# Order and engines of the last mixing steps in a fused attention, convolution and hierarchical MoE step

## The reference

```python
def hier_moe(h, w_rg, b_rg, w_re, b_re, w_gate, w_up, w_down):
    ...
    g_star = jnp.argmax(lg, axis=-1)                     # one of 4 groups per token
    ...
    top_p, top_i = lax.top_k(pe, TOP_K)                  # 2 of its 8 experts
    w = p_group * top_p / jnp.sum(top_p, axis=-1, keepdims=True)
    ...
    y = grouped_experts(x, e_idx, w.astype(x.dtype), w_gate, w_up, w_down)
    return y.reshape(b, t, d)

# grouped_experts: for the rows of each expert e
#   (silu(xblk @ w_gate[e]) * (xblk @ w_up[e])) @ w_down[e], times the token's weight, summed per token
# and the caller adds the residual: xp = xp + hier_moe(...), xs = xs + hier_moe(...)
```

## Time and profile before

| what | value |
|---|---|
| median of 3 runs | 1435.9 us (1434.64 to 1437.3) |
| the profiled execution's own time | 1436.35 us |
| its span, first to last instruction | 1434.4 us |
| PE (TensorE matmul) busy | 1242.1 us, 87% of the span |
| VectorE (DVE) busy | 433.2 us, 30% |
| ScalarE (ACT) busy | 217.4 us, 15% |
| bytes moved | 503.63 MB, mean 351 GB/s over the span |
| mean granted TensorE clock | 0.947 |

### The profile page before, as it was taken

The page is one execution under the profiler, slowest core; times in us unless marked ns, Lnnn a source line. Parts: engine busy times, 40 slices in busy tenths (PEclk is TensorE's granted clock), DMA queues, the critical chain, the costliest instruction groups (busy, mean ns, idle before and its releaser), DMA issues.

```text
span 1434.4 us, 21171 instructions
## 1 busy us (share of the span) xinstructions
PE 1242.1 (87%) x8998; PEld 675.9 (47%) x8998; DVE 433.2 (30%) x863; ACT 217.4 (15%) x462; POOL 45.4 (3%) x33
## 2 busy tenths in 40 slices
PE   9999999999999998997877778796787787777887
PEld 8888888888788862331222232132232122213223
DVE  4322127674211143322311321231222231132142
ACT  3111232322000043110101111011011010101101
POOL 0000003140000001000000000000000000000000
PEclk9999999999999999998989998899999898999899
DMA  9975443669399359999999999999999999999997
GB/s 342 348 227 183 140 133 121 206 206 340 88 349 413 121 182 427 417 425 435 427 433 432 430 433 431 431 431 431 431 432 432 430 432 432 432 432 430 433 426 317
DMA packets 101202, 503.63 MB, mean 351 GB/s; under 512 B 9294, under 2 KB 79638, under 8 KB 86182
## 3 DMA queue, kind: packets, MB, share of 16 engines
q1 hardware_dynamic: 89346, 494.86, 85.0%
q10 hardware_dynamic: 11812, 8.14, 1.8%
HBM read 496.42 MB, written 6.59 MB: 351 GB/s over the span
## 4 chain that ended last, share of the span: by engine, by line
PE 53%; DMA 44%; DVE 2%; ACT 1%; issue 0%; DVEq 0%; ACTq 0%; SPq 0%
PE bank L735 31%; DMA ring<-in_w_gate 16%; DMA ring<-in_w_up 15%; DMA ring<-in_w_down 12%; PE bank L1023 9%; PE bank L1058 3%; PE bank L958 2%; PE bank L1076 1%; DVE xa L1913 1%; PE bank L1073 1%; DMA xa<-in_x_prompt 1%; PE bank L746 0%; PE bank L826 0%; PE bank L776 0%; PE bank L1084 0%
## 5 line engine op out<-in xcount | busy, mean ns | idle before, releaser
L1023 PE MATMUL bank<-ring,bc 128*32 128x512 f32 x2040 | 272.4, 669 | 113.7 <-DMA ring<-in_w_gate 61.9
L735 PE MATMUL bank<-bc,ring 128*128 128x264 f32 x1536 | 350.8, 387 | 1.3 <-ACT cat L1261 1.3
L735 PEld LDWEIGHTS bank<-bc,ring 128*128 128x128 f32 x1536 | 288.2, 190 | 51.5 <-issue 2.3
L1023 PEld LDWEIGHTS bank<-ring,bc 128*32 128x32 f32 x2040 | 63.7, 118 | 288.2 <-issue 146.5
L1913 DVE TENSOR_TENSOR xa<-xa,bank 128x512 f32<-128x512 f32 x128 | 79.3, 682 | 153.0 <-PE bank L1076 146.6
L735 PE MATMUL bank<-cat,ring 128*128 128x264 f32 x512 | 114.9, 387 | 0.0
L735 PEld LDWEIGHTS bank<-cat,ring 128*128 128x128 f32 x512 | 97.0, 190 | 17.7 <-issue 1.3
L1927 DVE COPY bc<-bank 128x512 f32<-128x512 f32 x32 | 22.1, 691 | 234.6 <-PE bank L1023 234.6
L1058 PE MATMUL bank<-ring,cat 128*32 128x512 f32 x480 | 67.2, 684 | 22.4 <-DMA ring<-in_w_down 22.4
L958 PE MATMUL bank<-cat,bc 128*32 128x512 f32 x512 | 61.3, 597 | 13.5 <-DVE xa L1913 13.5
L1487 ACT ACTIVATE bc<-bank 128x512 f32<-128x512 f32 x32 | 19.1, 597 | 289.6 <-PE bank L1023 289.6
(11 more groups left out here) (300 smaller groups left out, 1023.5 us busy)
## 6 DMA issues: line engine op xcount, KB each, us to landing
ring<-in_w_gate SPq DMA_DIRECT2D x27, 4096.0 KB, 31.8
ring<-in_w_up SPq DMA_DIRECT2D x27, 4096.0 KB, 31.6
ring<-in_w_down SPq DMA_DIRECT2D x26, 4096.0 KB, 32.7
ring<-in_w_in SPq DMA_DIRECT2D x23, 2048.0 KB, 15.3
ring<-in_w_up SPq DMA_DIRECT2D x10, 2048.0 KB, 12.9
ring<-in_w_gate SPq DMA_DIRECT2D x9, 2048.0 KB, 15.4
ring<-in_w_down SPq DMA_DIRECT2D x9, 2048.0 KB, 16.1
ring<-in_w_out SPq DMA_DIRECT2D x8, 2048.0 KB, 16.5
```

Source lines behind the costliest of these rows:

```text
L735: m = pe.matmul(bank[n % 3][:, 0:T], w[:, k, (i % TPU) * P:(i % TPU + 1) * P], src[:, k, :], start=n_k == 0, stop=n_k == KT - 1)
L1023: m = pe.matmul(bank[b][c * C:(c + 1) * C, :], xeT[j % 2][:, k, :], wx, start=i == 0 and x < 4, stop=i == 1 and x >= 4, skip_group_check=True)
```

## The change

Four things are changed, the arithmetic aside from rounding order stays as it was.
- end_residual takes the half too. end_residual(1, 2) is taken from behind the third down's second half to ahead of it, and two new ones, (0, 0) and (0, 1), stand beside it. The pair (0, 0) so starts from the residual in its banks (END_ROWS).
- ScalarE moves the pair (0, 0) out of its banks with two plain copies (move_rows(0, 0), between its two copies of bank 2), as it does with (1, 1); VectorE's two adds of (0, 0) go. row_moved counts 4 per group, and the waits on it follow.
- mix_last(1) is split by t; sample_last(1) stands between its halves, and VectorE adds "s" ahead of both adds of (1, 0).
- The stores: SP issues the sample pieces 0, 1 and 2 ahead of y columns 1024 to 1535, which leave in one DMA of 512 KB; ScalarE's queue issues the sample piece 3 alone. There are eight DMAs in place of nine.

```diff
--- before.py
+++ after.py
@@ -131,9 +131,10 @@
 PIECE = 256
 END_BANKS = {(0, 0): 0, (0, 1): 6, (1, 0): 6, (1, 1): 3}
 END_ORDER = {0: (2, 3, 0, 1), 1: (0, 1, 2, 3)}
-END_ADDS = [(0, 1, 0), (0, 1, 1), (0, 0, 0), (0, 0, 1), (1, 0, 0), "s", (1, 0, 1)]
+END_ADDS = [(0, 1, 0), (0, 1, 1), "s", (1, 0, 0), (1, 0, 1)]
+END_ROWS = ((0, 0), (1, 1))
 END_ADD = {x: n + 1 for n, x in enumerate(END_ADDS)}
-END_MIX = {(0, 1): 1, (0, 0): 2, (1, 0): 3, (1, 1): 4, "s": 5}
+END_MIX = {(0, 1): 1, (0, 0): 2, "s": 3, (1, 0): 4, (1, 1): 5}
 NEND = len(END_ADDS)
 
 Y_ORDER = [(0, g) for g in range(4)] + [(1, g) for g in range(4)] + [(2, 0), (2, 1), None, (2, 2), (2, 3)]
@@ -646,20 +647,18 @@
 
             y = outs["y_prompt"].rearrange("o (t p) d -> p (o t) d", p=P)
             every = npass * (NG * NEND)
-            for n, last in ((1, (0, 1, 1)), (0, (0, 0, 1))):
-                cols = slice(512 * n, 512 * n + 512)
-                sp.wait_ge(end_added, every + END_ADD[last])
-                sp.dma_start(y[:, :, cols], xa[:, 0:2, cols]).then_inc(y_stored, 16)
+            sp.wait_ge(end_added, every + END_ADD[(0, 1, 1)])
+            sp.dma_start(y[:, :, 512:1024], xa[:, 0:2, 512:1024]).then_inc(y_stored, 16)
+            sp.wait_ge(row_moved, npass * (NG * 4) + 2)
+            sp.dma_start(y[:, :, 0:512], xa[:, 0:2, 0:512]).then_inc(y_stored, 16)
             cols = slice(1024, 1536)
             ys = outs["y_sample"].rearrange("b o (h g x) -> g (b o) h x", h=2, g=EG)
-            sp.wait_ge(end_added, every + END_ADD[(1, 0, 0)])
-            sp.dma_start(y[:, 0, cols], xa[:, 0, cols]).then_inc(y_stored, 16)
             sp.wait_ge(end_added, every + END_ADD["s"])
-            sp.dma_start(ys[0], halves(xa[0:NB, 2, 0:512])).then_inc(y_stored, 16)
+            for g in range(3):
+                sp.dma_start(ys[g], halves(xa[g * C:g * C + NB, 2, 0:512])).then_inc(y_stored, 16)
             sp.wait_ge(end_added, every + END_ADD[(1, 0, 1)])
-            sp.dma_start(y[:, 1, cols], xa[:, 1, cols]).then_inc(y_stored, 16)
-            sp.dma_start(ys[1], halves(xa[C:C + NB, 2, 0:512])).then_inc(y_stored, 16)
-            sp.wait_ge(y_stored, 144)
+            sp.dma_start(y[:, :, cols], xa[:, 0:2, cols]).then_inc(y_stored, 16)
+            sp.wait_ge(y_stored, 128)
             sp.wait_ge(state_stored, 16)
             sp.wait_ge(stored[0], STORED[0] + 16)
             sp.wait_ge(stored[1], STORED[1] + 16 * NB)
@@ -1089,11 +1088,11 @@
 
                     return bank[END_BANKS[(h, g // 2)] + g % 2]
 
-                def end_residual(g):
+                def end_residual(h, g):
 
                     for t in (0, 1):
-                        cols = slice(1024 + g * PIECE, 1024 + (g + 1) * PIECE)
-                        pe.matmul(end_bank(1, g)[:, t * PIECE:(t + 1) * PIECE], ident, xa[:, t, cols], start=t == 0, stop=False,
+                        cols = slice(h * 1024 + g * PIECE, h * 1024 + (g + 1) * PIECE)
+                        pe.matmul(end_bank(h, g)[:, t * PIECE:(t + 1) * PIECE], ident, xa[:, t, cols], start=t == 0, stop=False,
                                   skip_group_check=True)
 
                 def mix_third(h, gs):
@@ -1102,12 +1101,13 @@
                         for g in gs:
                             rows_ = slice(g * C, (g + 1) * C)
                             pe.matmul(end_bank(h, g)[:, t * PIECE:(t + 1) * PIECE], gateT[rows_, t, :], ye[rows_, h * PIECE:(h + 1) * PIECE],
-                                      start=t == 0 and (h, g // 2) != (1, 1), stop=False, skip_group_check=True)
-
-                def mix_last(h):
-
-                    pe.wait_ge(end_copied, it * 2 + h + 1)
-                    for t in (0, 1):
+                                      start=t == 0 and (h, g // 2) not in END_ROWS, stop=False, skip_group_check=True)
+
+                def mix_last(h, ts=(0, 1)):
+
+                    if 0 in ts:
+                        pe.wait_ge(end_copied, it * 2 + h + 1)
+                    for t in ts:
                         for g in END_ORDER[h]:
                             rows_ = slice(g * C, (g + 1) * C)
                             m = pe.matmul(end_bank(h, g)[:, t * PIECE:(t + 1) * PIECE], gateT3[rows_, t, :],
@@ -1146,7 +1146,7 @@
 
                     if j == 0:
                         pe.wait_ge(end_added, it * NEND + NEND)
-                        pe.wait_ge(row_moved, it * 2 + 2)
+                        pe.wait_ge(row_moved, it * 4 + 4)
                     gather((j + 1) % EG, it)
 
                 for j in range(EG):
@@ -1154,7 +1154,7 @@
 
                     pe.wait_ge(xe_ready, 2 * e + 1)
                     if j == 0:
-                        pe.wait_ge(end_added, it * NEND + END_ADD[(0, 0, 1)])
+                        pe.wait_ge(row_moved, it * 4 + 2)
                         unit_products(j, "g", 0)
                         unit_products(j, "u", 0)
                         pe.wait_ge(xe_ready, 2 * e + 2)
@@ -1197,15 +1197,18 @@
                         turn_gate(j)
                         continue
                     if j == EG - 1:
-                        end_residual(3)
+                        end_residual(1, 3)
                     if j >= 2:
                         adds_done((2, j - 2))
                     down(j - 1, 0, e)
                     turn_hidden(e)
+                    if j == EG - 1:
+                        end_residual(1, 2)
+                        end_residual(0, 0)
+                        end_residual(0, 1)
                     down(j - 1, 1)
 
                 e = it * EG + EG - 1
-                end_residual(2)
                 pe.wait_ge(xe_ready, 2 * e + 4)
                 pe.wait_ge(act_ready, e + 1)
                 pe.wait_ge(ye_copied, it * (EG - 1) + EG - 1)
@@ -1223,8 +1226,9 @@
                 sample_last(0)
                 pe.wait_ge(end_added, it * NEND + (NEND + END_ADD[(0, 1, 1)]))
                 mix_third(1, (0, 1))
-                mix_last(1)
+                mix_last(1, (0,))
                 sample_last(1)
+                mix_last(1, (1,))
 
             experts(0, True)
             pe.wait_ge(routed, 1)
@@ -1476,6 +1480,13 @@
                     A(gateT3 if j == EG - 1 else gateT, bank[5][:, 0:TT * P].rearrange("p (t s) -> p t s", t=TT), ACT.Copy
                       ).then_inc(gateT_copied, 1)
 
+                def move_rows(h, pair):
+
+                    act.wait_ge(end_mixed, it * len(END_MIX) + END_MIX[(h, pair)])
+                    b, c0 = END_BANKS[(h, pair)], h * 1024 + pair * 512
+                    for t in (0, 1):
+                        A(halves(xa[:, t, c0:c0 + 512]), psum[:, b:b + 2, t * PIECE:(t + 1) * PIECE], ACT.Copy).then_inc(row_moved, 1)
+
                 def copy_ye(e):
 
                     act.wait_ge(down_done, e + 1)
@@ -1503,12 +1514,10 @@
                               ).then_inc(x0_ready, 1)
                 act.wait_ge(end_down, it + 1)
                 A(g_sb[:, 0:PIECE], bank[2][:, 0:PIECE], ACT.Copy).then_inc(end_copied, 1)
+                move_rows(0, 0)
                 act.wait_ge(down_done, it * EG + EG)
                 A(g_sb[:, PIECE:2 * PIECE], bank[2][:, PIECE:2 * PIECE], ACT.Copy).then_inc(end_copied, 1)
-                act.wait_ge(end_mixed, it * len(END_MIX) + END_MIX[(1, 1)])
-                b = END_BANKS[(1, 1)]
-                for t in (0, 1):
-                    A(halves(xa[:, t, 1536:2048]), psum[:, b:b + 2, t * PIECE:(t + 1) * PIECE], ACT.Copy).then_inc(row_moved, 1)
+                move_rows(1, 1)
 
             experts(0, True)
             act.wait_ge(routed, 1)
@@ -1517,12 +1526,11 @@
                 experts(it, False)
 
             y = outs["y_prompt"].rearrange("o (t p) d -> p (o t) d", p=P)
-            act.wait_ge(row_moved, npass * (NG * 2) + 2)
+            act.wait_ge(row_moved, npass * (NG * 4) + 4)
             act.dma_start(y[:, :, 1536:2048], xa[:, 0:2, 1536:2048]).then_inc(y_stored, 16)
             ys = outs["y_sample"].rearrange("b o (h g x) -> g (b o) h x", h=2, g=EG)
             act.wait_ge(end_added, npass * (NG * NEND) + END_ADD["s"])
-            for g in (2, 3):
-                act.dma_start(ys[g], halves(xa[g * C:g * C + NB, 2, 0:512])).then_inc(y_stored, 16)
+            act.dma_start(ys[3], halves(xa[3 * C:3 * C + NB, 2, 0:512])).then_inc(y_stored, 16)
 
 
         @block.vector
@@ -1866,7 +1874,7 @@
             st.do(V.tensor_reduce(cpass, cwork, AX.X, ALU.add))
             V.memset(esum[:, 0:1], 0.0).then_inc(mix_added, NADDS)
             V.memset(esum[:, 1:2], 0.0).then_inc(mixed, NSTEPS)
-            V.memset(esum[:, 2:3], 0.0).then_inc(row_moved, 2)
+            V.memset(esum[:, 2:3], 0.0).then_inc(row_moved, 4)
             V.memset(esum[:, 3:4], 0.0).then_inc(end_added, NEND)
             V.tensor_copy(npass_sb[0:1, 0:1], cpass[0:1, :]).then_inc(routed, 1)
             first_gain(0)
@@ -1921,7 +1929,7 @@
                         if j >= 2:
                             for t in (0, 2, 1):
```

(2 more changed lines are left out.)

## The result

The changed kernel took 1447.45 us (median of 4 runs, 1446.7 to 1447.99), the kernel before 1436.6 us beside it; the ratio is 1.0074, interval 1.0062 to 1.0086. The prediction was 1435.3 us within 1433.4 to 1437.2. It is wrong by 12 us, and on the side to which it gave 4%.

The account below looks back on a forecast made before the run. The expert stage was taken as bound by the weight stream, so only the last group could pay: 0.9 us gained on PE, 0.3 given back to store order, 1435.9 - 0.6 = 1435.3 us, range 1433.4 to 1437.2.

Parts of the forecast that it names:

- the pricing of the added products: Groups 0 to 6: two more residual products add 1.9 us of PE to a group with 25 us spare, costing nothing.
- Its rival for a slower kernel: Every group: added residuals delay slot release and hold up the weight stream; 15 us added, 1451 us; chance 0.03.
- the prediction's own signs of being wrong: Loop GB/s fall, L1058 (third down's second half) stays at low clock, or tail behind PE's last matmul grows over 0.7 us.
- Residuals in the wait: Last group: three residuals before the third down's second half keep 2.4 GHz; half takes 1.92 us, mix_third starts 0.9 us earlier.
- What is late next: Last group: the last 1 MB lands at 1423.5, so the wait before end_products(1)'s second part caps the gain at about 1.1 us.
- ScalarE's move: End of last group: ScalarE's two copies of pair (0, 0), 1.08 us together, are hidden before its next job; costed at nothing.
- The tail: Behind PE's end: 0.3 of PE's 0.9 us given back to store order; span ends 0.6 us earlier, at 1433.7 to 1433.8.
- the large store ends it: Kernel's end: the 512 KB store issued last sets the end at 1435.0, 0.6 us later than now; 1436.5 us; chance 0.08.
- The sum: Whole kernel: span 0.6 us shorter, so 1435.9 - 0.6 = 1435.3 us.
- The range itself: Whole kernel: mechanism's ends 1434.7 to 1437.0, widened for run scatter of 1.3 us to either side to 1433.4 to 1437.2.

Follow-up runs that it names:

- e2: Changed kernel with the 13 warm-up products replaced by 4 wider ones, 36 fewer PE instructions ahead of the loop; 1437.18 us, ratio 1.0000.
- e3: Changed kernel with each residual product as one matmul of 512 columns instead of two of 256; 1438.19 us, ratio 1.0004.
- e1: Kernel before with 64 already satisfied waits on PE between group 0 and the loop, 32 more instructions, loop unchanged; 1447.01 us, ratio 1.0065.
- e7: Kernel before with 32 satisfied waits, its loop shifted by 16 PE instructions; 1447.52 us, one run.
- e8: Kernel before with 48 satisfied waits, its loop shifted by 24 PE instructions; 1447.79 us, one run.
- e5: Kernel before with only the residual product (1, 2) moved ahead of the third down's second half, none added; 1436.11 us, ratio 0.9991.
- e4: Changed kernel with each residual product as one 512-column matmul and the tail of the kernel before; 1435.58 us, ratio 0.9989.

## Why the prediction was wrong

- **The step that failed** is the pricing of the added products: "In groups 0 to 6 two more of them add 1.9 us of PE to a group that has 25 us spare: nothing". Of PE's time that is right; e2 and e3 have it and lose nothing that shows. But an instruction also has a place in the code. 15 more in the loop and 16 ahead of it pushed a loop that had at most 15 to spare over a boundary, 55 more fetches came, and the last group's work came 10.1 us later. The prediction had no term and no rival for it, though the queue row of the page (33 packets, none later than the first looped group) was there to be asked. Its rival for a slower kernel had the right victim, the stream, by a mechanism that e2 and e3 rule out. Two of the prediction's own signs of being wrong came true: 429 GB/s in the loop in place of 432, and a tail that grew by more than 0.7 us.
- **Residuals in the wait: right in the traces, with luck in the size.** Three took 2.86 us, the half 1.92 us, and mix_third came 1.04 us earlier against 0.9 forecast. All of that gain is against a half at the low clock. The prediction took the low clock as given by the wait of 2.1 us; in e1, e7 and e8 the same half after the same wait ran at the high one, and against them the three residuals cost some 0.35 us.
- **What is late next: right.** In the changed kernel the wait was 1.20 us, as the last loads came over half of the engines; in e5 it was 0.43 us, and in e2 none shows.
- **ScalarE's move: right at nothing.** e5 has the gain without it.
- **The tail: mis-sized.** 6.0 us behind PE's end were forecast, 6.8 measured, in the changed kernel as with the shifted loop. The issues came when they were forecast (the large one at 1430.37 us in e2, forecast about 1430.4). What was too small is the time from that issue to the span's end: 3.4 us forecast, 4.2 measured in both (1441.91 to 1446.1, 1430.37 to 1434.6). The rival "the large store ends it" said 4.6. The 1.2 us that the Trainium skill's page DMA: Bandwidth & Descriptors gives for a last store of 512 KB against one of 16 KB, in its section on the anatomy of one DMA, were nearer than the forecast: with the old tail (e4) 1431.58 to 1434.7 is 3.1 us, 1.1 less. That section is on transfers that GpSimd issues, and these are SP's.
- **The sum.** Without the fetches (e2) the change is worth 0.2 us more span or a ratio of 1.0000, where 0.6 us less was forecast: inside the range, and nothing that a run can tell. With them it costs 10.85 us by the medians. The range itself adds 1.3 us of scatter below but only 0.2 above; that made no difference here.

## What to carry to other kernels

Count a looped body's instructions as well as its engine time. When a long loop barely stays resident, as here with seven blocks of 256, a few more matmuls, even ones ahead of the loop, can make all of it be fetched again in every turn. The page's instruction queue row tells at once, and so does idle time "issue" at the loop's head. Beside a saturated stream the fetches cost bandwidth, not only a wait. Fewer, wider instructions for the same columns are then worth more than their own time, and two versions are compared only when both loops are resident or both are not. And before a gain is credited to a held clock, look at the same wait in several traces: one trace shows one of its two outcomes.

## What was not expected of the hardware

- The step: +16 instructions ahead of an unchanged loop, 33 to 88 fetches, 10 us. Moved by 160 it is gone again.
- One fetch of 16 KB took about 1.1 us of a DMA engine, and half of the engines ended late: 0.5 of the DMA share for 10 us at the end.
- 160 instructions of satisfied waits held PE for 17.6 us, 0.11 us each, and 32 of them (e1) for 3.2 us; as a filler they are not free.
- The length of a wait doesn't settle TensorE's clock. After 2.10 us the half ran at 1.2 GHz for most of its length; after 2.09 us in e1, and after 3.55 us in another group of the kernel before, it took the 1.92 us of 2.4 GHz.
